# A decoder layer on one core: squares of a tile in its own step and its rotation in the next, later chunk and sample steps, a shared evacuation, and a first FFN product ahead of the norm's sums

## Reference

```python
h = _rmsnorm(x, norm1_g)
z = jnp.einsum('btd,de->bte', h, w_in)
qa, ka, va, qm, km, vm, om, gif, ga, gb = jnp.split(z, offs, axis=-1)
qa = _rope_partial(_rmsnorm(qa.reshape(B, T, nh, HEAD_DIM), q_norm_g), pos)   # and ka
...
s = jnp.einsum('nbqhd,nbkhd->nbhqk', qb, kk) * (Dh ** -0.5)     # banded, three dilations
...
ya = jnp.einsum('bte,ed->btd', o_att, w_att_out)
hm = jax.nn.sigmoid(om) * h_m
yb = jnp.einsum('bte,ed->btd', hm, w_m_out)
mixed = jax.nn.sigmoid(ga) * ya + jax.nn.sigmoid(gb) * yb
x = x + jnp.einsum('btd,de->bte', mixed, w_o)
h = _rmsnorm(x, norm2_g)
ff = jax.nn.silu(h @ w_gate) * (h @ w_up)
return x + ff @ w_down
```

## Time and profile before

| | |
|---|---|
| median of 3 runs | 2390.24 us (2389.77 to 2395.87) |
| profiled execution, own time | 2388.5 us |
| its span, first to last instruction | 2386.6 us |
| PE busy | 2258.8 us (95%) |
| DVE, ACT, POOL busy | 938.7, 514.7, 681.7 us |
| mean granted TensorE clock | 0.967 of full speed |

### The profile page before, as it was taken

How to read it: one execution, slowest core, us unless ns; L and a number is a source line. 1 busy time by engine, 2 the same in 40 slices (tenths; PEclk the granted TensorE clock), 3 DMA queues, 4 the chain that set the end, 5 groups by cost and what they waited for, 6 DMA issues and landing times. The chain is left out here.

```text
span 2386.6 us, 34466 instructions
## 1 busy us (share of the span) xinstructions
PE 2258.8 (95%) x13972; PEld 2112.2 (89%) x13972; DVE 938.7 (39%) x1736; ACT 514.7 (22%) x1109; POOL 681.7 (29%) x662
## 2 busy tenths in 40 slices
PE   5999999999999998999699989899999999999998
PEld 4778898988977778999698879899999999999998
DVE  6664663466133322333234532325322323333224
ACT  4122553454233213333100010312000000000000
POOL 6213112221222312222221323325333233443310
PEclk8999999999999999999789899999999999999999
DMA  7215334434467735554755662423322233332201
GB/s 252 94 67 179 108 133 142 160 119 147 160 201 253 253 122 184 189 194 156 203 179 187 218 216 93 138 84 107 119 89 73 72 104 115 106 102 93 87 28 71
DMA packets 190123, 334.06 MB, mean 140 GB/s; under 512 B 42838, under 2 KB 98966, under 8 KB 187270
## 3 DMA queue, kind: packets, MB, share of 16 engines
q1 hardware_dynamic: 126008, 265.26, 34.0%
q10 hardware_dynamic: 63958, 66.62, 8.8%
HBM read 263.07 MB, written 156.81 MB: 176 GB/s over the span
## 5 line engine op out<-in xcount | busy, mean ns | idle before, releaser
L272 POOL CAST whi<-raw 128x512 fp32r<-128x512 f32 x324 | 248.8, 768 | 1584.4 <-PE ps L1871 513.5
L274 POOL TENSOR_TENSOR wlo<-raw,whi 128x512 fp32r<-128x512 f32 x324 | 440.9, 1361 | 33.5 <-issue 7.7
L285 PE MATMUL ps<-whi,hhi 128*128 128x512 f32 x832 | 345.3, 415 | 1.4 <-PEq L294 1.4
L287 PE MATMUL ps<-whi,hlo 128*128 128x512 f32 x832 | 333.3, 401 | 0.0
L286 PE MATMUL ps<-wlo,hhi 128*128 128x512 f32 x832 | 333.1, 400 | 0.0
L1871 PE MATMUL ps<-h2hi,whi 128*128 128x344 f32 x1056 | 225.1, 322 | 3.5 <-DVE h2lo L2395 3.5
L285 PEld LDWEIGHTS ps<-whi,hhi 128*128 128x128 f32 x832 | 207.8, 250 | 20.8 <-issue 1.8
L287 PEld LDWEIGHTS ps<-whi,hlo 128*128 128x128 f32 x832 | 207.7, 250 | 20.7
L286 PEld LDWEIGHTS ps<-wlo,hhi 128*128 128x128 f32 x832 | 208.8, 251 | 18.8
L1871 PE MATMUL ps<-h2lo,whi 128*128 128x344 f32 x1056 | 224.5, 321 | 0.0
L1871 PE MATMUL ps<-h2hi,wlo 128*128 128x344 f32 x1056 | 223.9, 320 | 0.0
(11 more groups left out here) (300 smaller groups left out, 3382.7 us busy)
## 6 DMA issues: line engine op xcount, KB each, us to landing
out<-in_cache_kv_w SPq DMA_DIRECT2D x144, 512.0 KB, 4.8
raw<-in_w_in SPq DMA_DIRECT2D x152, 256.0 KB, 4.7
a_tr<-tt SPq DMA_DIRECT2D x48, 256.0 KB, 2.1
out<-in_cache_kv_w SPq DMA_DIRECT2D x24, 508.0 KB, 4.9
raw<-in_w_gate SPq DMA_DIRECT2D x88, 128.0 KB, 2.1
raw<-in_w_up SPq DMA_DIRECT2D x88, 128.0 KB, 2.4
raw<-in_w_down SPq DMA_DIRECT2D x44, 256.0 KB, 3.6
gates<-e_sg ACTq DMA_DIRECT2D x16, 516.0 KB, 3.7
```

What stands on the lines that cost most here:

```text
L272: pool.tensor_copy(self.whi[:, p % RING, :], self.raw[:, p % RAW, :]).then_inc(self.w_hi, 1)
L274: pool.tensor_tensor(self.wlo[:, p % RING, :], self.raw[:, p % RAW, :], self.whi[:, p % RING, :].bitcast(F32), ALU.subtract).then_inc(self ...
L285: nc.tensor.matmul(out, lhs[0], rhs[0], start=start, stop=False)
L287: return nc.tensor.matmul(out, lhs[1], rhs[0], start=False, stop=stop)
```

## The change

Five edits. In `project`, DVE makes the squares of tile u at the end of step u (a function of its own, before the scores) and rotates tile u - 1 in step u; ACT's root stands ahead of the exponentials. In `gate_projections`, the chunks begin at segment 3 instead of 1, and chunks 5 to 7 instead of only chunk 7 go without a free segment. In `output_gates`, all steps of `SampleSoftmax` come seven segments later. In `output_projection`, ACT copies the even pieces of the turned input and DVE the odd ones. In `ffn`, the matmuls with ones stand behind the first gate product, and DVE takes their result behind the low halves.

```diff
@@ Projection @@
         v = u - 1
         if self.valid(v) and self.normed(v):
-            dve.wait_ge(self.ev, v + 1)
-            squares(dve, ch, self.zt[:, v % Z, :], self.sq[:], self.st[:, v % Z, :], P).then_inc(self.var, 1)
-        v = u - 2
-        if self.valid(v) and self.normed(v):
             g, x, n = self.kind(v)
             dve.wait_ge(self.std, self.normed_to[v] + 1)
             rotate(...)
+
+    def dve_squares(self, u):
+
+        dve, z = self.core.nc.vector, u % self.Z
+        if self.valid(u) and self.normed(u):
+            dve.wait_ge(self.ev, u + 1)
+            squares(dve, self.core.dve, self.zt[:, z, :], self.sq[:], self.st[:, z, :], P).then_inc(self.var, 1)
@@ project @@
                 proj.act_turned(u)
+                proj.act_root(u)
                 att.act_exp(u)
                 att.act_take(u)
-                proj.act_root(u)
...
                 proj.dve_new(u)
+                proj.dve_squares(u)
                 att.dve_scores(u)
@@ gate_projections @@
-    PER = 6
+    FIRST, PER, WIDE = 3, 6, 5
...
-            n, r = divmod(i - 1, PER)
-            if n == NT - 1:
-                return n * chunks.STEPS + r if r < chunks.STEPS else None
-            return None if r == 1 or n < 0 else n * chunks.STEPS + max(r - 1, 0)
+            i -= FIRST
+            if i < 0:
+                return None
+            if i >= WIDE * PER:
+                return WIDE * chunks.STEPS + i - WIDE * PER
+            n, r = divmod(i, PER)
+            return None if r == 1 else n * chunks.STEPS + max(r - 1, 0)
@@ output_gates @@
-        parts = [GroupMerge(core, c), SampleSoftmax(core, c)]
+        parts = [(GroupMerge(core, c), 0), (SampleSoftmax(core, c), 7)]
...
-                for part in parts:
-                    part.pe(i)
+                for part, first in parts:
+                    if i >= first:
+                        part.pe(i - first)
@@ output_projection, DVE @@
+                for v in range(u * HALF, (u + 1) * HALF) if u < 2 else ():
...
+                    if v % 2:
+                        dve.wait_ge(tr, v + 1)
+                        nc.vector.tensor_copy(acc[...], ps[:, 7, :]...).then_inc(xt[1], 1)
@@ ffn, PE @@
-            for s in range(3):
-                last = nc.tensor.matmul(ps[:, 3 + s, 0:SEG], core.ones[:], rs[:, s * SEG:(s + 1) * SEG],
-                                        start=True, stop=True)
-            last.then_inc(tot, 1)
             for i, (kind, j, m) in enumerate(order):
                 if i == 1:
+                    (the same three matmuls)
+                    last.then_inc(tot, 1)
                     pe.wait_ge(var, 1)
@@ ffn, DVE @@
-            dve.wait_ge(tot, 1)
-            nc.vector.tensor_scalar(seg3(rs[:]), ps[:, 3:6, 0:SEG], 1.0 / D, EPS, ALU.mult, ALU.add).then_inc(var, 1)
             for k in range(KD):
                 dve.wait_ge(nhi, k + 1)
                 nc.vector.scalar_tensor_tensor(lo[:, k, :], acc[:, k, :], core.g2[:, k:k + 1], ...)
+            dve.wait_ge(tot, 1)
+            nc.vector.tensor_scalar(seg3(rs[:]), ps[:, 3:6, 0:SEG], 1.0 / D, EPS, ALU.mult, ALU.add).then_inc(var, 1)
```

More of the change, by code:

```diff
@@ L2027, in _ @@
         def _(pool):
-            parts[1].pool()
+            parts[1][0].pool()
             core.split_weights(core.taken + 8)
@@ L2043, in _ @@
                 u, s = divmod(i, 3)
-                for part in parts:
-                    part.act(i)
+                for part, first in parts:
+                    if i >= first:
+                        part.act(i - first)
                 if s == 1 and u + 1 < KD:
@@ L2060, in _ @@
                     act.dma_start(core.hm_t[u, :, 0:S], hm[:, u % 2, :]).then_inc(out[u % 2], 16)
-            for part in parts:
+            for part, _ in parts:
                 part.act_end()
@@ L2070, in _ @@
                 u, s = divmod(i, 3)
-                for part in parts:
-                    part.dve(i)
+                for part, first in parts:
+                    if i >= first:
+                        part.dve(i - first)
                 cols = slice(s * SEG, min((s + 1) * SEG, S))
@@ L2174, in output_projection @@
         units = Groups(core, "o_mm", 2, KD)
-        his, los, tr, xt, ev, sqd, sum_sq = (sem(f"o_{x}") for x in ("his", "los", "tr", "xt", "ev", "sq", "sum"))
+        his, los, tr, ev, sqd, sum_sq = (sem(f"o_{x}") for x in ("his", "los", "tr", "ev", "sq", "sum"))
+        xt = [sem("o_xt_act"), sem("o_xt_dve")]
         x_in = [sem(f"o_xin{i}") for i in range(4)]
@@ L2209, in _ @@
                 cols = P if n < NT else NB
[L2210 to L2213, removed]
+                if v % 2 == 0:
+                    act.wait_ge(tr, v + 1)
+                    nc.scalar.activation(acc[:, 4 * kk:4 * kk + 4, n * P:n * P + cols],
+                                         ps[:, 6, :].rearrange("p (k c) -> p k c", k=4)[:, :, 0:cols],
+                                         ACT.Copy).then_inc(xt[0], 1)
             for u in range(KD):
@@ L2231, in _ @@
             for u in range(KD):
+                for v in range(u * HALF, (u + 1) * HALF) if u < 2 else ():
+                    n = v % HALF
+                    cols = P if n < NT else NB
+                    if v % 2:
+                        dve.wait_ge(tr, v + 1)
+                        nc.vector.tensor_copy(acc[:, 4 * u:4 * u + 4, n * P:n * P + cols],
+                                              ps[:, 7, :].rearrange("p (k c) -> p k c", k=4)[:, :, 0:cols]).then_inc(xt[1], 1)
                 units.wait(dve, u)
-                dve.wait_ge(xt, HALF if u < 4 else 2 * HALF)
+                dve.wait_ge(xt[0], HALF // 2 + 1 if u < 4 else HALF)
+                dve.wait_ge(xt[1], HALF // 2 if u < 4 else HALF)
                 nc.vector.tensor_tensor(seg3(acc[:, u, :]), seg3(acc[:, u, :]), banks(core, u), ALU.add).then_inc(ev, 1)
@@ L2249, in _ @@
                     if v >= 2:
-                        pe.wait_ge(xt, v - 1)
+                        pe.wait_ge(xt[v % 2], v // 2)
                     for k in range(4):
@@ L2328, in _ @@
         def _(pe):
-            for s in range(3):
-                last = nc.tensor.matmul(ps[:, 3 + s, 0:SEG], core.ones[:], rs[:, s * SEG:(s + 1) * SEG],
-                                        start=True, stop=True)
-            last.then_inc(tot, 1)
             for i, (kind, j, m) in enumerate(order):
                 if i == 1:
+                    for s in range(3):
+                        last = nc.tensor.matmul(ps[:, 3 + s, 0:SEG], core.ones[:], rs[:, s * SEG:(s + 1) * SEG],
+                                                start=True, stop=True)
+                    last.then_inc(tot, 1)
                     pe.wait_ge(var, 1)
```

## The result

| | before | changed |
|---|---|---|
| median, us | 2390.7 | 2351.7 |
| lowest to highest, runs | 2389.8 to 2395.9, 4 | 2348.8 to 2354.4, 4 |
| profiled execution, own time, us | 2388.5 | 2350.6 |

The ratio of the times is 0.983, with a 95% interval of 0.981 to 0.985: faster by 1.7%, or 39 us. The forecast was 2341, the range 2330 to 2356: the time lies in the range, 10.7 us above the forecast.

What follows compares the result with a forecast made beforehand. The prediction took TensorE (PE) to bound the kernel, busy 2258.8 of 2386.6 us. Its terms, -41.1 + 0.4 - 7.7 - 0.5 - 0.5 = -49.4 us from 2388.5, gave 2339.1, adjusted to the median as 2341 us; range 2330 to 2356.

Steps and rivals of the forecast that it cites:

- Part 1: `project`, squares and rotation reordered: 27.2 us of PE's rotation waits and 13.9 us of half clock go, -41.1 us.
- With no wait there is nothing that makes the clock fall: `project`: with the six long waits gone, the 13.9 us lost to lowered clock behind them are won back.
- The exponentials: `project`, attention's exponentials behind root and table load: up to 2.5 us later, 0.7 us of cover left, costed at nothing.
- The rule of the Trainium skill: `project`: about 1.38 us of drain per table switch, so 0.7 us waits at six short units, gain 4 us smaller.
- Part 2: `gate_projections`, chunks two segments later: PE's 6.15 us load wait becomes a wait for ACT's first sigmoid, +0.4 us.
- Chunks 5 and 6 without a free segment: `gate_projections`: these would be like chunk 7, where PE has no wait over 0.2 us, so no cost.
- Part 3: `output_gates`, sample softmax later: PE's 13.03 us wait for `s_z` goes, a 5.4 us wait remains, -7.7 us.
- if the issue begins 2 us behind segment 4: `output_gates`: condition under which issuing the merge weights' loads ends at 1173.1, leaving 3.4 us for their landing.
- the wait of `output_gates` moves: Rival: the merge chain, once covered by the 13 us, makes PE wait behind segment 6; 2349 us, chance 0.10.
- Part 4: `output_projection`, two engines for the turned input: PE's 1.8 us wait for ACT's copies can go, input DMAs limit, -0.5 us.
- part 5: FFN start, first gate product ahead of the ones products: DVE's low halves 3.7 us sooner, 3.2 us given back, -0.5 us.
- the last rival: `project`, exponentials late everywhere, costing 48 us per us past the cover; 2395 us at 1.15 us a step, chance 0.04.

Runs made afterwards that it cites:

- chunk_loads_late: Changed kernel, with the six loads of chunk 1 in `gate_projections` issued by ACT behind its second sigmoid instead of ahead of its first: 2344.5 us, ratio 0.980.
- part3_sample: Kernel before, with only the steps of `SampleSoftmax` in `output_gates` seven segments later: 2391.1 us, ratio 0.9988.
- after_again: The changed kernel, unedited, run again for the scatter of one program: 2352.4 us, ratio 0.983.
- merge_one_later: Changed kernel with chunk 1's loads behind ACT's second sigmoid, the merge's first ten loads issued by SP, and merge products one segment later: 2333.5 us, ratio 0.976.
- before_again: The kernel before, unedited, run again for the scatter of one program: 2392.4 us, ratio 1.0000.
- part 1 alone: Kernel before, with only the `project` edits: squares in the tile's own step, rotation one step on, root ahead of the exponentials: 2352.0 us, ratio 0.983.
- parts245: Changed kernel with the `project` and `SampleSoftmax` edits taken back, leaving later chunks, two engines for the turned input and the FFN start: 2397.7 us, ratio 1.0017.

## Why the prediction was right or wrong

**Part 1, -41.1: right.** All eight waits are gone. Against the one profile of before that I had, `project` gained 38.1; that profile lost 15.6 us to half clock, and three others without part 1 lost 19 to 21. Against the mean of the four (848.5, 851.7, 852.5, 851.1: 850.9) it is 40.6. "With no wait there is nothing that makes the clock fall" held: 1.00 from 45 to 849 us.

**The exponentials, "I cost it at nothing": right.** ACT and PE of the changed kernel at the only item where PE waited for them. This is an early item, and no short unit of the kind that I had worked out shows any:

```profile
222.54 0.21 ACT L573 ACTIVATE st<-st 128x8 f32<-128x8 f32 x1 [4.45 <-DVE st L651]
...
222.77 1.28 ACT L854 ACT_TABLE_LOAD   x1
224.07 0.41 ACT L854 ACTIVATE sc<-sc,nm 128x128 f32<-128x128 f32 x1
...
225.77 0.65 PE L811 MATMUL ps<-ident,sc 128*128 128x128 f32 x4 [0.59 <-ACT sc L854]
```

0.6 us once, not 48 times. The table load starts 0.02 us after the root's end, and the exponential 0.02 us after the load's 1.28 us, as the root did behind its own load in the earlier trace rows. The rule of the Trainium skill that I weighed (page "ScalarE: Activation LUTs", section "What ACT_TABLE_LOAD costs", some 1.38 us of drain beside the load) would have put a further gap there and a wait at each short unit; neither is seen, so the row decided rightly.

**Part 2, +0.4: mechanism right, size too small.** Four profiles with the old places have 251.3, 250.6, 250.6 and 250.7 (mean 250.8), five with the new ones and the chunk loads unmoved 252.3, 252.4, 252.6, 252.7 and 254.5 (mean 252.9): +2.1, and +1.1 in the first pair. ACT and PE of the changed kernel at the stage's start:

```profile
852.31 0.97 ACTq L1341 DMA_DIRECT2D c_mb<-neg_all  x2
...
861.14 0.46 ACTq L1347 DMA_DIRECT2D c_v<-m_tok  x1
861.63 1.28 ACT L1993 ACT_TABLE_LOAD   x1 [16.17 <-issue]
862.92 0.81 ACT L1993 ACTIVATE e_sg<-ps 128x344 f32<-128x344 f32 x2
...
863.43 0.65 PE L285 MATMUL ps<-hhi,whi 128*128 128x344 f32 x1 [3.30 <-ACT e_sg L1993]
```

ACT issues the twelve loads from 852.31 to 861.60, 9.3 us. (Its idle time of 16.17 us, counted from its last activation, holds the change of stage as well.) Then PE goes on the moment the first sigmoid is through. I had about 6.6 us for this wait (897.0 to 903.6); it was 3.3 here and 4.7 to 6.4 in four others. The cause is shown: chunk_loads_late removes it. What I missed is the second half: "Chunks 5 and 6 without a free segment are like chunk 7 now [...] Nothing." PE waits there for ACT's `c_num`, 0.2 to 2.1 us in the profiles with the new places. A caution on the size: the wait that part 2 was to remove was 6.15 us in the profile that I read, but 3.4 to 4.9 in the three others with the old places and ACT's loads unmoved.

**Part 3, -7.7: this step failed in size.** In the pair of profiles it is -3.7. Over all profiles with ACT's loads unmoved, five with part 3 have a mean of 176.1 (174.8, 175.7, 178.2, 175.4, 176.4) and four without it 178.4: -2.3. The two groups touch (178.2 is the longest with part 3, 177.8 the shortest without), so no single pair of profiles shows it. ACT and PE of the changed kernel in the stage:

```profile
1109.17 5.20 ACTq L1090 DMA_DIRECT2D ml<-ml_nat  x6
1114.40 2.05 ACTq L1083 DMA_DIRECT2D og<-o_grp  x4
1116.49 0.46 ACT L2064 ACTIVATE v_sg<-ps 128x344 f32<-128x344 f32 x1 [20.19 <-issue]
...
1128.36 6.21 ACTq L1099 DMA_DIRECT2D cf_nat<-cf  x3
...
1135.87 0.46 ACT L2064 ACTIVATE v_sg<-ps 128x344 f32<-128x344 f32 x1 [8.51 <-issue]
...
1138.42 2.36 ACTq L1104 DMA_DIRECT2D cr<-cf_nat  x4
...
1117.00 0.66 PE L285 MATMUL ps<-hhi,whi 128*128 128x344 f32 x1 [4.39 <-ACT v_sg L2064]
...
1136.38 0.43 PE L285 MATMUL ps<-hhi,whi 128*128 128x344 f32 x1 [1.96 <-ACT v_sg L2064]
...
1142.09 1.97 PE L1158 MATMUL ps<-ident,cr 128*64 128x128 f32 x32 [1.67 <-DMA cr<-cf_nat]
```

The first wait is the one that I forecast, 4.4 for 5.4 us (5.5 to 6.8 in the four others). What failed is the condition "if the issue begins 2 us behind segment 4", as it did before (1177.35 to 1179.29). Segment 4 ended at 1130.64 and the issue began at 1138.42, 7.8 us behind it. The landing itself needed only 1.3 us from the end of the issue, of the "3.4 us [...] left". Three stores of the merge stand in front of that issue, which awaits their landing; they kept ACT for 6.21 us and landed at 1138.40. By them a sigmoid came 2.0 us late, and the weights 1.7 us late (3.2 in part3_sample). Some 40 us later, where merge and sample steps overlap, DVE's `at` cost PE another 2.0; part3_sample and after_again don't have that wait. The 13 us wait gave way to waits that add up to 10.0. This is the rival "the wait of `output_gates` moves", with most of the loss elsewhere than behind segment 6: the named wait was only the last of the chain. That ACT's loads begin this chain is shown (168.3 us on average without them). That one segment more removes the wait for the weights is shown by merge_one_later, that it shortens the stage is not.

**Part 4, -0.5, and part 5, -0.5: both nothing.** ACT's 1.8 us shrank to 0.4, and the input's DMAs (3.2 + 0.6) and DVE (0.4) make it 4.6 in all. Before, with the 2.4 us that PE already waited for the input's DMAs, it was 4.2; "the input's DMAs [...] are what PE meets" was right, and it left no gain. In the FFN the wait for `var` (`sumsq L2416`), forecast as 1.3, was 1.3, and 8.0 us ahead of the first product go to the low halves (`h2lo`). The stages of both together take 876.5 to 879.8 with the two parts (nine profiles) and 876.3 to 877.2 without (four): no gain. What each of the two does by itself was not run.

**The balance.** The forecast had 0.60 on its own range of 2335 to 2347, and that was missed. 2351.7 lies nearest to "the wait of `output_gates` moves" (2349, chance 0.10), but only 4.0 of the 11.5 us are that rival's. That the time lies in the wide range is owed to part 1, 41 of the 49 us, which was right. Own time to own time the forecast was -49.4 and the result -37.9. Of the 11.5 us between them, 3.0 lie in `project` and 2.3 in the stage behind `output_gates`, both within the scatter of one program (3.2 and 2.9 between before and before_again); 4.0 in part 3, 0.7 in part 2, 1.5 in parts 4 and 5 and their stages. By medians part 1 alone gave 2352.0 and the whole change 2351.7 and 2352.4: what part 3 wins (2.3 by the stages), part 2 costs (2.1), though these sums are smaller than the times can resolve. That parts245 should lose 4 us stays open: its profile is of the fastest of its ten runs, and the span there (2389.1) lies between those of the two profiles of before (2386.6 and 2393.6). Open too is why the same program took 174.8 and 178.2 us in `output_gates`; the longer one waited 3.6 us for `cr`, the other 1.7, and 11.4 us for `f_lo` at its end, the other 9.6.

Two small slips of the working: 903.60 less 903.13 is 0.5, not 0.4, in part 2, and the last rival's 1.15 us a step comes to 2396, not 2395.

## What to carry to other kernels

When an engine's in-order list holds work for two tiles, ask for each piece whose deadline comes first: the rotation did not have to get faster (5.1 and 4.9 us), it stood behind squares that had to wait for a newer tile, and moving them gave the whole gain, a third of it through the clock. A wait at a stage's start that you cover by starting later moves to whatever the issuing engine does next: count the DMA instructions that stand ahead of an activation as work of that engine, and move them off it (some 13 us here for two stage starts). Before crediting a part with a few us, take a second profile of the same kernel; a stage without any edit moved by 3 us.

## What I had not expected of the hardware

The clock scatters between executions of one program: `project` of before lost 15.6 us to half clock in one profile and 20.8 in the other, with the same waits (27.2 and 27.4). The stage behind `output_gates` takes 78.2 to 79.2 us in five profiles and 80.3 to 81.2 in the eight others, whatever the kernel, with nothing between. What sets it apart was not tried.

A DMA's issue costs its engine very different times. The three stores `cf_nat<-cf` took 6.21 us of ACT after the change (above) and 3.25 before, and from 1.9 to 6.2 over all profiles:

```profile
1173.55 3.25 ACTq L1095 DMA_DIRECT2D cf_nat<-cf  x3
```

The DMA share was 0.98 in the 6.21 us and 0.90 in the 3.25 us; what the stores met was not tried. Ten loads at the start of `output_gates` hold ACT for 7.3 us (1109.17 to 1116.45), and the twelve chunk loads of `gate_projections` for 9.3 us, ahead of its first sigmoid there.
